# A two-layer hybrid encoder step on one core: how the first expert gets its rows, where the attention scores lie, and the order of the first transfers

## The reference, cut to what matters

```
def diff_core(q, k, v, lam, mask):
    s = jnp.einsum('bqhcd,bkhcd->bhcqk', q, k, preferred_element_type=F32) * (D_C ** -0.5)
    ...
    p = jax.nn.softmax(s, axis=-1)
    a = p[:, :, 0] - lam * p[:, :, 1]
    return jnp.einsum('bhqk,bkhe->bqhe', a, v.astype(F32))

def moe_ffn(x, w_r, wg, wu, wd):
    xt = x.reshape(-1, D)
    logits = jnp.dot(xt, w_r, preferred_element_type=F32)
    top_v, top_i = lax.top_k(logits, TOP_K)
    w = jax.nn.softmax(top_v, axis=-1)
    gates = jnp.einsum('tk,tke->te', w, jax.nn.one_hot(top_i, N_EXPERTS, dtype=F32))
    for e in range(N_EXPERTS):
        h = jax.nn.silu(xt @ wg[e]) * (xt @ wu[e])
        y = y + gates[:, e:e + 1] * jnp.dot(h, wd[e], preferred_element_type=F32)
```

## Time and profile before

| | us |
|---|---|
| median of 3 runs (lowest to highest) | 1617.64 (1616.2 to 1619.38) |
| profiled execution | 1617.72 |
| its span | 1615.8 |
| PE busy in the span | 1556.8 (96%) |
| DVE busy | 1245.6 (77%) |
| ACT busy | 1002.1 (62%) |
| POOL busy | 212.7 (13%) |
| mean granted TensorE clock | 0.983 |

### The profile page before, as it was taken

How to read it: one execution, slowest core, us unless ns; L and a number is a source line. 1 busy time by engine, 2 the same in 40 slices (tenths; PEclk the granted TensorE clock), 3 DMA queues, 4 the chain that set the end, 5 groups by cost and what they waited for, 6 DMA issues and landing times.

```text
span 1615.8 us, 21783 instructions
## 1 busy us (share of the span) xinstructions
PE 1556.8 (96%) x8454; PEld 1351.2 (84%) x8454; DVE 1245.6 (77%) x1303; ACT 1002.1 (62%) x1078; POOL 212.7 (13%) x269
## 2 busy tenths in 40 slices
PE   6999989999999995999999999999999999999996
PEld 4988989999998895788888888888888888888885
DVE  4766666663567564998998898898898998898995
ACT  3554543333446443677777777777777777777774
POOL 4802320000051131000100100100101001002000
PEclk9999999999999996999999999999999999999998
DMA  5532444444434237999999999999999999999992
GB/s 157 148 105 79 91 136 156 157 157 155 132 109 138 68 99 216 315 359 366 380 393 370 375 386 376 378 395 364 383 383 372 384 381 375 381 390 367 382 384 89
DMA packets 222434, 437.45 MB, mean 271 GB/s; under 512 B 11649, under 2 KB 65741, under 8 KB 222333
## 3 DMA queue, kind: packets, MB, share of 16 engines
q1 hardware_dynamic: 214944, 420.64, 73.2%
q0 software_dynamic: 5984, 12.28, 2.7%
q10 hardware_dynamic: 1404, 3.15, 0.6%
HBM read 428.52 MB, written 13.28 MB: 273 GB/s over the span
## 4 chain that ended last, share of the span: by engine, by line
PE 90%; DVE 3%; ACT 2%; DMA 2%; POOL 1%; issue 1%; ACTq 0%; POOLq 0%; DVEq 0%
PE bank L1820 30%; PE bank L2278 13%; PE bank L2283 13%; PE bank L2279 13%; PE bank L2289 6%; PE bank L2292 6%; PE bank L2298 6%; PE bank L1823 2%; PE bank L2307 2%; ACT cut_hi L843 1%; DMA ring<-ffn_w_up 1%; DVE cut_lo L1212 1%; POOL acc L643 1%; DMA xhat<-x_sample 1%; DMA ring<-w_in 0%
## 5 line engine op out<-in xcount | busy, mean ns | idle before, releaser
L1756 DVE TENSOR_TENSOR split_lo<-raw,split_hi 128x2048 fp32r<-128x2048 f32 x336 | 766.8, 2289 | 96.8 <-ACT split_hi L1119 95.9
L1119 ACT CAST split_hi<-raw 128x2048 fp32r<-128x2048 f32 x336 | 640.1, 1910 | 232.9 <-PE bank L2283 142.5
L2278 PE MATMUL bank<-split_hi,xgT_hi 128*128 128x512 f32 x896 | 354.5, 396 | 2.6 <-DVE xgT_lo L1767 2.6
L2279 PE MATMUL bank<-split_hi,xgT_lo 128*128 128x512 f32 x896 | 350.2, 391 | 0.0
L843 ACT CAST cut_hi<-ring 128x1024 fp32r<-128x1024 f32 x124 | 129.6, 1048 | 203.2 <-PE bank L1820 197.1
L1212 DVE TENSOR_TENSOR cut_lo<-ring,cut_hi 128x1024 fp32r<-128x1024 f32 x124 | 153.4, 1239 | 132.4 <-ACT cut_hi L843 132.2
L1820 PE MATMUL bank<-xT_hi,cut_hi 128*128 128x320 f32 x752 | 243.6, 324 | 5.1 <-DVE cut_lo L1212 2.1
L2283 PE MATMUL bank<-split_lo,xgT_hi 128*128 128x512 f32 x896 | 240.9, 391 | 0.0
L1820 PE MATMUL bank<-xT_hi,cut_lo 128*128 128x320 f32 x752 | 235.1, 313 | 0.0
L1820 PE MATMUL bank<-xT_lo,cut_hi 128*128 128x320 f32 x752 | 235.1, 313 | 0.0
L2278 PEld LDWEIGHTS bank<-split_hi,xgT_hi 128*128 128x128 f32 x896 | 168.8, 188 | 36.9 <-DVE xgT_lo L1767 3.0
(11 more groups left out here) (286 smaller groups left out, 1625.8 us busy)
## 6 DMA issues: line engine op xcount, KB each, us to landing
raw<-moe_w_gate SPq DMA_DIRECT2D x112, 1024.0 KB, 9.3
raw<-moe_w_up SPq DMA_DIRECT2D x112, 1024.0 KB, 9.2
raw<-moe_w_down SPq DMA_DIRECT2D x112, 1024.0 KB, 7.2
ring<-w_in SPq DMA_DIRECT2D x16, 1024.0 KB, 5.2
ring<-ffn_w_gate SPq DMA_DIRECT2D x11, 1024.0 KB, 5.6
ring<-ffn_w_up SPq DMA_DIRECT2D x11, 1024.0 KB, 5.4
ring<-ffn_w_down SPq DMA_DIRECT2D x10, 1024.0 KB, 5.1
ring<-w_out SPq DMA_DIRECT2D x8, 1024.0 KB, 5.1
```

Of the source, the lines that this page charges most:

```text
L1119: return nc.scalar.copy(split_hi[:, i % SR, :], raw_piece(i)).then_inc(hi_ready, 1)
L1756: V.tensor_tensor(split_lo[:, i % SR, :], raw_piece(i), split_hi[:, i % SR, :].bitcast(F32), ALU.subtract).then_inc(lo_ready, 1)
L2278: TE.matmul(o, xgT_hi[:, kk, :], hi[:, c], start=kk == 0, stop=False)
L2279: TE.matmul(o, xgT_lo[:, kk, :], hi[:, c], start=False, stop=False)
```

## The change

It has three parts, and all of them touch the programs of several engines.

1. **First transfers.** ACT's queue now issues the first unit of `w_in` behind the tokens, and no longer the 24 gain rows and the large table of constants; SP issues those, with the four `prow` tables that POOL had. ACT and DVE cut the first weight unit, then start on the tokens, and cut the second and third units between and behind them.
2. **Scores.** The two halves go to two banks (`bank45`) and stand next to each other in PE's program; a head's scores wait until the head before has been read. ACT's and DVE's cuts of an iteration stand earlier in it.
3. **Routing and the first expert.** Expert 0's rows are no longer gathered: 24 float32 products of the token rows with the one-hot table `Gown` put them, transposed, into four banks. Its slot weights come from three small products (`own,Gown`) ahead of piece 2. The slot table of all experts is made by POOL: six indirect transfers write one row of 16 bytes (token, scale, gate) for each token and choice to its slot's place in DRAM, and one transfer reads the table back as `slots`. DVE makes the indices from it (`places`) at piece 16 of expert 0. The 24 tables `G`, `late_members` and `late_tokens` are gone. The first three weight pieces are cut before the routing's copies and squares.

```
-        banks = [ctx.enter_context(nc.psum_tensor(f"bank{i}", [P, 512], F32)) for i in range(8)]
+        banks = [ctx.enter_context(nc.psum_tensor(f"bank{i}", [P, 512], F32)) for i in range(4)]
+        score_banks = ctx.enter_context(nc.psum_tensor("bank45", [P, 2, 512], F32))
+        banks += [score_banks[:, 0], score_banks[:, 1]]
+        banks += [ctx.enter_context(nc.psum_tensor(f"bank{i}", [P, 512], F32)) for i in (6, 7)]
+
+        scores_of = score_banks[:, :, 0:256]
...
+        x0_banks = [banks[4], banks[5], banks[2 + (RT.n[("rk",)]) % 2], banks[2 + (RT.n[("cnt",)]) % 2]]
...
+            sp.wait_ge(prow_zero, 1)
...
+            for w, name in enumerate(("g_gla", "g_sub")):
+                for k, a, b, d in ((0, 0, 96, 0), (0, 96, 128, 0), (1, 0, 64, 32), (1, 64, 128, 0), (2, 0, 32, 64), (2, 32, 128, 0)):
+                    for l in range(DEPTH):
+                        r = 6 * w + 3 * l + k
+                        sp.dma_start(prow2[r:r + 1, a:b], A[name][l:l + 1, d:d + b - a]).then_inc(gains_in, 16)
             for n, u in enumerate(UNITS):
-                if n == 1:
+                if n == 0:
                     sp.wait_ge(x_in, 32)
+                    continue
                 if n == 2:
+                    sp.dma_start(const[:, P:CONST_W], A["const"][:, P:CONST_W]).then_inc(const_in, 16)
...
-            act.dma_start(const[:, P:CONST_W], A["const"][:, P:CONST_W]).then_inc(const_in, 16)
+            act.dma_start(ring[:, 0, 0:SLOT].rearrange("p (b n) -> p b n", b=KB),
+                          A["w_in"][0][:, KC:KC + 256].rearrange("(k p) n -> p k n", p=P)).then_inc(ring_full[0], 16)
...
-            for q in range(CR):
-                hi(q)
+            hi(0)
             for o in range(KB):
                 x_hi(0, o)
                 x_square(0, o)
+                if o == 4:
+                    hi(1)
+            hi(2)
...
-            for q in range(2):
-                lo(q)
-            for o in range(KB):
+            residual(0, 0)
+            dve.wait_ge(RT.free, RT.emptied(("par",)))
+            lo(0)
+            for o in range(1, KB):
                 residual(0, o)
-                if o:
-                    x_lo(0, o - 1)
+                x_lo(0, o - 1)
+                if o == 5:
+                    lo(1)
...
-                    s = RS.bank(("s", l, n)).rearrange("p (c k) -> p c k", c=2)
+                    s = scores_of
...
+                    if n:
+                        hi(q0 + Q_FILL + n + 2)
...
-                    RS.begin(pe, ("s", l, n))
                     if n % H == 0:
                         pe.wait_ge(RT.free, RT.emptied(("qt", l, n // H)))
-                    first_half = step.mark(scores(n, 0))
+                    pe.wait_ge(RS.free, RS.n["s", l, n])
+                    scores(n, 0)
+                    scores(n, 1).then_inc(RS.full, 1)
                     if n >= 2:
                         differ_T(n - 2)
                     if n >= 3:
                         attended(n - 3)
-                    step.wait(first_half)
-                    scores(n, 1).then_inc(RS.full, 1)
...
+                pe.wait_ge(RS.free, RS.emptied(("s", l, HEADS - 1)))
...
+            pool.wait_ge(table_zero, 16)
+            pool.wait_ge(tags_ready, 1)
+            for t, (t0, rows) in enumerate(TILES):
+                for k in range(2):
+                    pool.indirect_dma_start(out=table[:, :], out_offset=bass.IndirectOffsetOnAxis(ap=row_of[0:rows, t, k:k + 1], axis=0),
+                                            in_=tags[0:rows, t, k, :], in_offset=None).then_inc(table_out, 16)
+            pool.wait_ge(table_out, 16 * 2 * NT)
+            pool.dma_start(slots[:].rearrange("p n c -> p (n c)"), table.rearrange("(p n) c -> p (n c)", p=P)).then_inc(table_in, 16)
...
+            first_hi(0)
+            first_hi(1)
+            x_copy(RS, 2, 0)
+            first_hi(2)
+            act.wait_ge(RC.free, RC.emptied(("wo", 1, WO_RING.rindex("C"))))
+            act.wait_ge(k_out, 16 * 3 * DEPTH)
+            x_copy(RC, 0, 1)
+            x_copy(RC, 1, 1)
+            row_squares(0)
+            x_copy(RC, 2, 1)
+            row_squares(1)
+            row_squares(2)
...
-            xg_hi(0, 0)
+            for g in range(4):
+                act.wait_ge(x0_full, g + 1)
+                for k in (2 * g, 2 * g + 1):
+                    last = nc.scalar.activation(xgT_hi[:, k, :], x0_banks[g][:, 128 * (k % 2):128 * (k % 2) + 128], ACT.Copy, scale=gcol(3)[:, k:k + 1])
+                last.then_inc(x0_hi, 1)
+            act.nop().then_inc(th_ready, 2)
+            act.wait_ge(gate_in, 1)
+            nc.scalar.activation(gd[:, :, 1:2], gd[:, :, 0:1], ACT.Exp).then_inc(gate_out, 1)
...
+            step(V.tensor_tensor(picked[:], oh[:], rank[:].unsqueeze(2).to_broadcast([P, NT, 2, NE]), ALU.mult))
+            step(V.tensor_reduce(at_rank[:], picked[:], AX_X, ALU.add))
+            step(V.scalar_tensor_tensor(out=row_f[:], in0=at_rank[:], scalar=float(MAXB * NE), in1=topf[:, :, 0:2], op0=ALU.mult, op1=ALU.add))
+            for b in range(1, MAXB):
+                step(V.tensor_scalar(beyond[:], at_rank[:], float(P * b), float(NE - P * MAXB * NE), ALU.is_ge, ALU.mult))
+                step(V.tensor_tensor(row_f[:], row_f[:], beyond[:], ALU.add))
+            V.tensor_copy(row_of[:], row_f[:])
...
+            def x0_lo(g):
+
+                dve.wait_ge(x0_hi, g + 1)
+                for k in (2 * g, 2 * g + 1):
+                    last = V.scalar_tensor_tensor(out=xgT_lo[:, k, :], in0=x0_banks[g][:, 128 * (k % 2):128 * (k % 2) + 128], scalar=gcol(3)[:, k:k + 1],
+                                                  in1=xgT_hi[:, k, :].bitcast(F32), op0=ALU.mult, op1=ALU.subtract)
+                if g % 2:
+                    last.then_inc(t_free, 1)
...
-                    if done and 6 <= i < 6 + NE:
-                        late_members(i - 6)
+                    if done and i == SR + 1:
+                        own_weights()
                     if done and i == 8 + NE:
-                        slots(RO, ("idxB",), NE, (MAXB - 1) * NE)
+                        places()
...
+            for g in range(4):
+                if g == 3:
+                    pe.wait_ge(RT.free, RT.count)
+                for k in (2 * g, 2 * g + 1):
+                    o = x0_banks[g][:, 128 * (k % 2):128 * (k % 2) + 128]
                     for t, (t0, rows) in enumerate(TILES):
-                        last = mm(out(s)[:, 0:width], members(t, s)[0:rows], tag[0:rows, t, e, 0:width], t == 0, t == NT - 1)
-                return last
-
-            pe.wait_ge(G_ready, 1)
-            b0 = RT.begin(pe, ("idx0",))
-            tokens_of(0, lambda t, s: G[:, 0, t], [0], lambda s: b0, 2).then_inc(RT.full, 1)
-            pe.wait_ge(RS.free, RS.count)
-            bA = RD.begin(pe, ("idxA",))
-            pe.wait_ge(tag_ready, 1)
-            for e in range(NE):
-                pe.wait_ge(G_ready, e + 1)
-                last = tokens_of(e, lambda t, s: G[:, e, t], [0], lambda s: bA[:, 8 * e:8 * e + 8], 8)
-            last.then_inc(RD.full, 1)
-            pe.wait_ge(xg_in, 16)
-            xg_T(0, None)
-
-            pe.wait_ge(RC.free, RC.count)
-            pe.wait_ge(RT.free, RT.count)
+                        last = mm(o, x[0:rows, t, P * k:P * k + P], Gown[0:rows, t, :], t == 0, t == NT - 1)
+                last.then_inc(x0_full, 1)
+            pe.nop().then_inc(t_full, 2)
...
+                    if first and i == 2:
+                        b = RD.begin(pe, ("own",))
+                        pe.wait_ge(own_ready, 1)
+                        for t, (t0, rows) in enumerate(TILES):
+                            last = mm(b[:, 0:2], Gown[0:rows, t, :], own[0:rows, t, :], t == 0, t == NT - 1)
+                        last.then_inc(RD.full, 1)
```

More of the change, by code:

```diff
@@ L238, in build @@
     hx = nc.dram_tensor("token_rows", (T, D), F32, kind="Internal").ap()
+    table = nc.dram_tensor("slot_table", (P * MAXB * NE, 4), F32, kind="Internal").ap()
     with ExitStack() as ctx:
@@ L408, in build @@
         gd = sb("gd", [P, NT, 4])
-        gatew = sb("gatew", [P, NT, NE])
-        gatew2 = sb("gatew2", [P, NT, NE])
-        rest = sb("rest", [P, NT, NE])
         rrow = sb("rrow", [P, NT, 1])
[L413 to L417, removed]
+        picked = sb("picked", [P, NT, 2, NE])
+        at_rank = sb("at_rank", [P, NT, 2])
+        row_f = sb("row_f", [P, NT, 2])
+        beyond = sb("beyond", [P, NT, 2])
+        row_of = sb("row_of", [P, NT, 2], U32)
+        tags = sb("tags", [P, NT, 2, 4])
+        own = sb("own", [P, NT, 2])
+        own1 = sb("own1", [P, NT, 1])
+        slots = sb("slots", [P, MAXB * NE, 4])
+        Gown = sb("Gown", [P, NT, P])
         away = sb("away", [P, MAXB * NE])
         spot = sb("spot", [P, MAXB * NE])
-        slot_w = sb("slot_w", [P, MAXB * NE, 2])
         now_w = sb("now_w", [P, 2, 2])
@@ L1156, in experts @@
                     piece_hi(i)
```

(28 more changed lines are left out.)

206 lines of the change are left out of this document (82 added, 124 removed).

## The result

The change made the kernel slower: 1626.86 us in the median of five runs (1622.71 to 1627.18) against 1617.64 before, a ratio of 1.0047 with a 95% interval of 1.0029 to 1.0065 (ratios here come from all timed runs of both kernels, so they differ a little from the quotient of the two medians). I had forecast 1585. The profiled execution took 1622.71, with a span of 1620.9.

The account below looks back on a forecast made before the run. PE was taken to bound the kernel, busy 1556.8 of 1615.8 us. Terms of -6 (first transfers), -9 (scores) and -18 (routing) sum to -33 from 1617.72, forecasting 1585, with a range of 1576 to 1602.

Parts of the forecast that it names:

- This stretch is no part of the change.: Experts' steady stretch: PE busy at full clock, 2.79 us an expert's piece, taken as untouched by the change.
- my rival with the late table: Slot table returns too late in expert 0, stalling DVE at piece 16, then PE; 1626 at 12.5 us a scatter; chance 0.03.
- Part 1, -6 us: Start: reordered first transfers bring the first product to 13.5 us, 7.4 earlier, less 1.2 for DVE's second cut; bounds -8 to -3.
- Part 2, -9: Heads of both layers: adjacent score halves save 6.1 us a layer less a 1.4 tail; -2 if they don't overlap.
- The overlap: Heads: two score halves on different partitions run together, so the second is free, saving 6.1 us of PE a layer.
- The cost against it: Heads: a longer tail behind the last head, from two cuts ahead of the last exponentials' readers, 1.4 us a layer.
- The wait on the single pair of banks: Heads: scores wait until the head before is read, with 2.7 us of cover; costed at nothing; as a stalling rival, chance 0.03.
- Part 3, -18: Routing and expert 0: piece 0 starts 10.4 us earlier, runs 2.2 faster, tables save 5.6 net; bound -13 at low clock.
- The tables of expert 0: Expert 0: dropping its tables saves 6.0 us over 14 pieces, less under 0.5 for three small products.
- the wrong branch: Routing: the clock rises after 4.7 us of the `Gown` products, the remaining 29 take 0.15 us each, ending at 635.7.
- The rival with the low clock: Routing: the clock stays low through the `Gown` products, so that part gives -13 and the total 1590; chance 0.25.
- The table's round trip: Expert 0: scatters and reading back of the slot table finish at 663 to 670 us, ahead of DVE's need near 672.

Follow-up runs that it names:

- run 1: The change plus two unused pads restoring the experts' tiles to their earlier offsets modulo 512 bytes: 1603.61 us, ratio 0.990 to the kernel before.
- run 2: The kernel before, with unused pads putting the experts' six tiles at the change's addresses: 1642.38 us, ratio 1.0135.
- run 5: PE-only kernel, none of the reference's work: the experts' product pattern with weights shifted against moving data in 32-byte steps; 0.2275 to 0.2340 us a product.
- run 7: The change with the two offset-restoring pads, its scores part undone: 1604.6 us, ratio 0.9932 to the kernel before.
- run 8: The change with the two offset-restoring pads, plus 12 unused 512-column products ahead of the `Gown` products: 1598.95 us, ratio 0.9886 to the kernel before.
- run 9: The change with offset-restoring pads and 12 unused 512-column products, plus pads aligning the layers' moving tiles to 256 bytes: ratio 0.9884 to the kernel before.

## Why the prediction was wrong

**"This stretch is no part of the change."** This step failed, and it decided the sign. I took the experts' stretch as given, because no instruction in it was edited. Its pace hangs on the distance of two tiles in memory, and the change moved them. It was worth +22 us (runs 1, 2 and 5), and the same move cost some 3 more in the layers. With the distance mended the change is 1% faster, 0.990, and ends on the side that I forecast, with half of the gain: 16 us in place of 33. The measured 1626.86 stands next to the 1626 of my rival with the late table. That is chance, for the table was there 16 us before DVE came to it.

**Part 1, -6 us; measured -1.6** at the first head, nothing in the ratio. The step on ACT's queue was right, done at 5.8 us (I had 5.5). What I put at 10 us, the landing of the first weight unit, was 12.43; then the second cut opened a wait of 2.11 us inside the first group, for which I had 1.2.

**Part 2, -9; measured -5** (run 7). The overlap was right: PE's work fell by 5 us a layer, some 6.6 at an equal clock, and I had 6.1. The cost against it was mis-sized and in another place, 2.2 to 2.6 us a layer in place of 1.4, some of it in waits for `am` and `att` inside the loop that I had costed at nothing. The wait on the single pair of banks, also costed at nothing, took 0.38 and 1.56 us in the trace of the change and nothing in run 1.

**Part 3, -18; measured** (646.08 - 616.18) - (634.34 - 609.61) = 5.2 us up to piece 0, and (772.97 - 646.08) - (758.04 - 634.34) = 3.2 in expert 0, to which 2.7 of the slower pace are to be added: -11. The tables of expert 0 were worth about what I said: of the 5.9 us piece 0 gives 5.03 - 4.46 = 0.6, which leaves 5.3 against 5.6. For the clock I took the wrong branch, and with it the price of the 48 instructions: 14.96 us in place of 9.1. "As nothing sets these products apart from the pieces but their width" was no reason: the clock did not rise in their 14.96 us, and it rose within piece 0. Whether it was their width, or that they are float32 and the pieces float32r, no run tells. The rival with the low clock had the event right, but its price of 0.243 us for an instruction was scaled from 288 columns, and it took 0.312. Run 8 shows the other branch: with the clock raised beforehand an instruction took 0.174.

**The table's round trip** was right: back near 662.6, where I had 663 to 670, and needed at 679.11.

The Trainium skill's sentence on transposes that I had set beside this (TensorE: Matmul & The Clock Gate, Part 4: PE-mode transpose) did not help: these products are not transposes, and the clock did not come up with them either.

## What to carry to other kernels

Where PE is the bound, the offset of its weights against its moving data is a parameter of the kernel: for 512 float32r columns keep it a multiple of 256 bytes (for 320 columns moving data 192 above the weights' offset were slightly better), and measure it afresh whenever a tile is added or resized. An edit's cost is not confined to the instructions that it touches; compare the start-to-start distance of the commonest instruction before anything else. If PE has small products ahead of a long stretch, check the granted clock there, and whether dense work can raise it first; here that was worth 2 to 4 us. And once a loop waits for other engines, as the heads do after the change, less work on PE no longer shortens it.

## What the runs showed of the hardware

A 512-column float32r product costs 0.2275 us when the weights lie 0 bytes from the moving data modulo 256, 0.2290 at 192, and 0.2332 to 0.2340 at every other multiple of 32 (run 5). Why 192 lies between is open. The Trainium skill (TensorE: Matmul & The Clock Gate, Part 2, Back-to-back issue gap) gives columns / 2.4 + 2.5 ns at full clock for a product by itself, which is 216 ns here, and some 131 ns for each product of 512 columns in a stream of weight loads and products. The best setting of run 5, such a stream in float32r, shows 227, so neither figure holds here, and the page has no term for where the operands lie. With the same instructions the whole kernel differs by 1.4% between two placements (run 2).

Float32 products of 128 columns left the clock at 1.2 GHz for 14.96 us, 48 instructions in a row in the change, and kept it at 2.4 GHz for 8.35 us once it was there (run 8; run 9 shows the same).
